# Where a planner puts 224 small modulation tiles among the weight turns of a two-block transformer kernel

## The chip, the cores and the metric

The kernel runs on one core of a Trainium2 chip. The metric is the device time of one execution in microseconds. The three runs of the kernel before took 2783.18, 2784.40 and 2785.71 us, median 2784.4 us. One profiled execution gives the trace that the text reads.

## The reference

Two transformer blocks run one after the other on 256 tokens of width 2048, all in float32. What matters here is the first block's gating and output, and the modulation vectors that both blocks need:

```python
shift, scale, gate = split(silu(c) @ w_ada + b_ada, 3)          # block 1
q, k, v, z_a, u_b, z_b, g_a, g_b = h @ w_in                      # 76 column tiles of 128
y = (sigmoid(g_a) * ((attn * silu(z_a)) @ w_pa)
     + sigmoid(g_b) * ((fourier(u_b) * silu(z_b)) @ w_pb)) @ w_out
x = rmsnorm(x + gate * y)
shift1, scale1, gate1, shift2, scale2, gate2 = split(silu(c_2) @ w_mod + b_mod, 6)   # block 2
...                                                              # block 2: projections, two kinds of attention, merge, feed-forward
```

`gate` (2048 columns) and the six vectors of block 2 are products of one vector with a 2048 x 2048 matrix each. Seven such matrices are 112 MB of weights.

## The kernel before

Activations lie feature-major in SBUF. Each weight matrix is cut into column tiles of 128, and the work is a list of **turns** (867 of them): a turn loads up to 8 weight tiles of 128 x 128 (512 KB) into one of 7 raw buffers, ScalarE (ACT) rounds them to a high part (`hi_turn`, tile `whi`, 5 buffers), VectorE (DVE) subtracts to get the low part (`lo`, tile `wlo`, 4 buffers), and TensorE (PE) multiplies both with the activations. A weight column of 16 k-tiles takes two turns; it is a **unit** with a name (`q`, `za`, `ga`, `pa`, ...). When a unit ends, ACT copies one half of its PSUM bank out (`taken`) and DVE adds the other half (`join`); only then may the unit that next uses that bank start (`claim` on PE). The banks 7 and 6 alternate from unit to unit.

The modulation matrices don't go through PE. DVE multiplies each 128 x 1024 piece by a scalar per partition and adds it into `acc` (`mod_tile`); 32 such tiles, in the order of k, make one vector, and 224 make all seven. After the last of a vector, PE sums over the partitions (`m_sum`, in the turn `plan.sums` names) and DVE folds the result into `mod`, in one burst of small instructions.

`Plan.place_mods` decides in which turn each tile lies. Every turn has a rate, the first argument of `single`; the planner adds the rates up, and each time the credit reaches one, a tile goes into that turn. After a sum it leaves a gap of three turns. The list of loads follows that order: the weights of turn t, then the tiles placed in t. Loads go out on the SP queue one by one, each into the raw buffer that the load **seven before it** used, so SP waits until DVE has finished with that one. A turn's load and a modulation tile each take one of the seven buffers.

The engines are in order. For each t the queues do this, where it touches the change:

- ACT, iteration t: `taken` of units that ended in turn t-1; then `hi_turn(t + 3)`, which waits for that load to land; then tanh and others.
- DVE, iteration t: `join` of units that ended in t-1; the fold of a vector whose sum was in t-1; `mod_tile` for the tiles placed in t+1; `lo` of turn t+2; then the gating arithmetic.
- PE, turn t: the `whi` products, small products of attention and others, the sum if there is one, the `wlo` products.

In the merge (turns 74 to 177) a loop of seven turns repeats: `ga` in two turns, `gb` in two, `pa` in two of 6 tiles each, `pb` in one of 4 tiles. The text calls them g1, g2, g3, g4, a1, a2 and b. `pa` uses the same bank as the `ga` that follows it, so g1 of the next loop can start only when `pa` has been joined, and between the end of `pa` and that start there is only turn b.

Of the kernel before, what the change touches and what calls it, by code (L numbers as in the profile page):

```python
# [147 lines left out]
class Plan:  # L148
# [18 lines left out]
    def single(self, rate, name, i, bank, rhs, weights, pieces, kt0=0, **more):  # L167
        u = Unit(name, i, bank, rhs, range(kt0, kt0 + sum(pieces)), **more)
        k = 0
        for p in pieces:  # L170
            self.turn(rate, weights[:, 128 * k:128 * (k + p)], [(u, kt0 + k + x) for x in range(p)])
            k += p
        self.finish(u)
# [18 lines left out]
    def build(self):  # L192
        src, single = self.src, self.single
        w1, w2, wp = src["w1"], src["w2"], src["w_proj"]
        two = (8, 8)
        ring = itertools.cycle((7, 6))
        bank = lambda: next(ring)
        single(0, "v", 3, bank(), "both", w1[19], two, wide=True)
        for h in range(12):
            single(.66 if h > 1 else 0.2, "q", h, bank(), "x1", w1[h], two)  # L200
            single(.66 if h > 1 else 0.2, "za", h, bank(), "x1", w1[20 + h], two)
        for g in range(4):
            single(.8, "ub", g, bank(), "x1", w1[32 + g], two)
            single(.8, "zb", g, bank(), "x1", w1[36 + g], two)

        def gates(n):
            single(.5, "ga", n, bank(), "x1", w1[40 + n], two)
            single(.5, "gb", n, bank(), "x1", w1[56 + n], two)

        gates(0)  # L210
        gates(1)
        for n in range(16):
            single(.37 if n < 15 else 0, "pa", n, bank(), "w", wp[n, :, 0:1536], (6, 6))
            single(.25 if n < 15 else 0, "pb", n, bank(), "w", wp[n, :, 1536:2048], (4,), kt0=12)
            if n + 2 < 16:
                gates(n + 2)
        for n in range(16):
# [2083 lines left out]
```

How the kernel before makes its waits and increments, by code:

```python
    def wait_ge(self, signal, value):  # L71
        return self
# [17 lines left out]
    def wait_ge(self, signal, value):  # L90
        if self.seen.get(signal, 0) < value:
            self.seen[signal] = value
            self.e.wait_ge(signal, value)
# [409 lines left out]
    def sp(e):  # L503
        e.dma_start(COLS[:, :], src["cols"]).then_inc(*lands("cols_in", "cols"))
        e.dma_start(K1[:, 0:256], src["k1"][:, 0:256]).then_inc(*lands("k1_in", "k1"))
        for i, kts in enumerate((slice(0, 2), slice(2, 6), slice(6, 10), slice(10, 14), slice(14, 16))):
            e.dma_start(XC[:, kts, :], src["xc"][:, kts, :]).then_inc(*lands(f"xc_in{i}", "xc", i))
        for r, (source, cols, shape, label) in enumerate(LOADS):
            if r >= NR:
                e.wait_ge(*on(*LOADS[r - NR][3]))
            o = raw(r)[:, 0:cols]
            if shape:
                o = o.rearrange("p (a b) -> p a b", a=shape)
            e.dma_start(o, source).then_inc(*lands(f"raw_in{r % NR}", "landed", r))
            if r == n_start - 1:
                e.dma_start(K1[:, 256:], src["k1"][:, 256:]).then_inc(*lands("k1_rest", "k1_rest"))
        for n in range(12, 16):
            e.wait_ge(*on("stored", n))
        e.wait_ge(*on("spilled"))
# [5 lines left out]
        def claim(b):  # L525
            for label in held[b]:
                e.wait_ge(*on(*label))
# [8 lines left out]
        def scale_rows(j, tiles):  # L537
# [1 line left out]
            c = 128 * GROUPS[j][1]  # L539
            if j > 1 and tiles[0] == 0:
                e.wait_ge(*on("cols_taken", j - 2 if j == 2 else j - 1))
            for i in tiles:
```

## Time and profile before

| | |
|---|---|
| median of three runs | 2784.4 us (2783.18 to 2785.71) |
| profiled execution, own time | 2783.18 us |
| its span, first to last instruction | 2781.4 us |
| around the span | 1.8 us |
| PE busy | 2757.3 us, 99% |
| DVE busy | 2049.0 us, 74% |
| ACT busy | 1458.6 us, 52% |
| granted clock of PE | 0.999 |

The span is what the trace's times are made of; a change of the span is added to the time.

### The profile page before, as it was taken

What the parts mean: (1) busy time and instruction counts of PE and PEld (TensorE: products, weight loads), DVE (VectorE), ACT (ScalarE), POOL (GpSimd) and SP (SyncE); (2) the same over time, 40 slices, a digit from 0 to 9 for tenths busy, and PEclk for the clock granted to TensorE, in tenths of its full rate; (3) what the DMA queues carried; (4) which work ended last, traced back from release to release, by engine and by line L of the source; (5) the groups of instructions that cost most, each with busy time, mean ns of one, the idle gap of its engine ahead of it and who ended that gap; (6) DMA issues with size and microseconds to landing.
All of it is one profiled execution on the core that took longest, in us unless ns stands there. A gap on an engine that the chain in (4) does not pass through costs nothing.

```text
span 2781.4 us, 42932 instructions
## 1 busy us (share of the span) xinstructions
PE 2757.3 (99%) x16354; PEld 2382.8 (86%) x16354; DVE 2049.0 (74%) x3589; ACT 1458.6 (52%) x2414; POOL 375.9 (14%) x958
## 2 busy tenths in 40 slices
PE   8999999999999999999999999999999999999999
PEld 4778888888888888888888888888888888888888
DVE  4468877878988787887878887778978555555554
ACT  3465544555566666666666444545454443444443
POOL 0014300000002424344343310000000000000000
PEclk9999999999999999999999999999999999999999
DMA  9956778888866555555555778888858555555564
GB/s 360 353 167 228 228 247 260 271 287 294 279 187 193 166 173 178 177 184 175 174 176 180 225 240 271 311 286 273 278 171 296 190 186 187 191 187 191 182 198 142
DMA packets 183582, 621.84 MB, mean 224 GB/s; under 512 B 20288, under 2 KB 28752, under 8 KB 182736
## 3 DMA queue, kind: packets, MB, share of 16 engines
q1 hardware_dynamic: 173360, 605.62, 66.1%
q10 hardware_dynamic: 10016, 13.47, 1.5%
q8 instruction: 130, 2.13, 0.3%
q14 instruction: 76, 0.62, 0.1%
HBM read 612.70 MB, written 4.21 MB: 222 GB/s over the span
## 4 chain that ended last, share of the span: by engine, by line
PE 87%; DVE 5%; ACT 3%; POOL 3%; issue 1%; DMA 1%; ACTq 0%; SPq 0%; DVEq 0%
PE ps L96 86%; POOL small L111 2%; DVE wlo L111 1%; POOL small L114 1%; PE ps L99 1%; DVE c_y L117 1%; ACT sb_l L102 1%; ACT whi L102 0%; DMA raw<-in_w_s 0%; ACT L105 0%; DMA xc<-in_xc 0%; DVE acc L117 0%; ACT sb_z L102 0%; DVE i_t L111 0%; DMA q_sw<-q_g 0%
## 5 line engine op out<-in xcount | busy, mean ns | idle before, releaser
L96 PE MATMUL ps<-act,whi 128*128 128x512 f32 (+1 forms) x6560 | 1657.4, 392 | 0.7 <-DVE act L111 0.7
L96 PEld LDWEIGHTS ps<-act,whi 128*128 128x128 f32 (+1 forms) x6560 | 1176.3, 188 | 216.2 <-issue 5.7
L111 DVE TENSOR_TENSOR wlo<-raw,whi 128x1024 fp32r<-128x1024 f32 (+3 forms) x883 | 1040.4, 1185 | 22.6 <-ACT whi L102 18.2
L102 ACT ACTIVATE whi<-raw 128x1024 fp32r<-128x1024 f32 (+3 forms) x883 | 893.9, 1027 | 194.9 <-PE ps L96 101.8
L96 PE MATMUL ps<-act,wlo 128*128 128x256 f32 (+2 forms) x6416 | 971.8, 290 | 0.0
L96 PEld LDWEIGHTS ps<-act,wlo 128*128 128x128 f32 (+1 forms) x6416 | 868.6, 190 | 55.8 <-issue 9.2
L117 DVE SCALAR_TENSOR_TENSOR acc<-raw,c_act,acc 128x1024 f32<-128x1024 f32 x210 | 268.2, 1277 | 0.0
L114 POOL TENSOR_SCALAR small<-small 128x2 f32<-128x2 f32 (+3 forms) x316 | 134.4, 425 | 937.6 <-DVE small L114 808.9
L111 POOL TENSOR_TENSOR small<-small 128x2 f32<-128x2 f32 (+1 forms) x460 | 162.7, 354 | 348.2 <-ACT u_u L102 314.0
L111 DVE TENSOR_TENSOR w_u<-w_u,ps 128x256 f32<-128x256 f32 x44 | 18.4, 420 | 95.2 <-ACT w_u L102 95.2
L117 DVE SCALAR_TENSOR_TENSOR h_res<-ps,mod,h_res 128x256 f32<-128x256 f32 x64 | 30.8, 483 | 68.3 <-PE ps L96 67.2
L111 DVE TENSOR_TENSOR w_g<-w_g,ps 128x256 f32<-128x256 f32 x44 | 18.3, 420 | 85.2 <-ACT w_g L102 85.2
L102 ACT ACTIVATE w_g<-ps 128x256 f32<-128x256 f32 x44 | 16.7, 384 | 120.7 <-PE ps L96 120.7
L102 ACT ACTIVATE w_u<-ps 128x256 f32<-128x256 f32 x44 | 16.8, 384 | 120.3 <-PE ps L96 120.3
L111 POOL TENSOR_TENSOR small<-small,small 128x4 f32<-128x4 f32 (+1 forms) x160 | 74.8, 467 | 13.1
L96 PE MATMUL ps<-m_act,whi 128*128 128x512 f32 x256 | 64.4, 393 | 1.0 <-DVE m_act L117 1.0
L96 PEld LDWEIGHTS ps<-m_act,whi 128*128 128x128 f32 x256 | 46.0, 189 | 9.6 <-DVE m_act L117 1.4
L117 DVE SCALAR_TENSOR_TENSOR d_o<-ps,mod,h_res 128x256 f32<-128x256 f32 x16 | 7.7, 483 | 58.4 <-PE ps L96 58.4
L96 PE MATMUL ps<-ff_act,whi 128*128 128x512 f32 x192 | 49.4, 392 | 0.0
L111 DVE TENSOR_TENSOR i_x<-i_x,ps 128x128 f32<-128x128 f32 x96 | 27.2, 283 | 28.0 <-PE ps L96 27.8
L117 DVE SCALAR_TENSOR_TENSOR c_y<-x_p,cols,c_y 128x256 f32<-128x256 f32 x96 | 45.8, 477 | 2.3
L102 ACT ACTIVATE x_p<-ps 128x256 f32<-128x256 f32 x48 | 18.4, 384 | 53.5 <-PE ps L96 37.9
(328 smaller groups left out, 2298.3 us busy)
## 6 DMA issues: line engine op xcount, KB each, us to landing
raw<-in_w SPq DMA_DIRECT2D x418, 512.0 KB, 4.9
raw<-in_w_mod SPq DMA_DIRECT2D x192, 512.0 KB, 4.7
raw<-in_w_gate SPq DMA_DIRECT2D x88, 512.0 KB, 4.4
raw<-in_w_up SPq DMA_DIRECT2D x88, 512.0 KB, 4.4
raw<-in_w_s SPq DMA_DIRECT2D x64, 512.0 KB, 6.6
raw<-in_w_out SPq DMA_DIRECT2D x64, 512.0 KB, 5.9
raw<-in_w_down SPq DMA_DIRECT2D x64, 448.0 KB, 4.5
raw<-in_w_ada SPq DMA_DIRECT2D x32, 512.0 KB, 5.2
```

The lines of the kernel that those rows point to most:

```text
L96: return self.e.matmul(*args, **more)
L99: return self.e.transpose(*args)
L102: return self.e.activation(*args, **more)
L111: return self.e.tensor_tensor(*args)
L114: return self.e.tensor_scalar(*args)
L117: return self.e.scalar_tensor_tensor(*args, **more)
```

## The change

The rates of the turns before the first output projection are replaced by one number, 0.58. The rates of the first ten turns and of `pa`, `pb` number 15 stay. No instruction is added or removed: 224 tiles, 7 sums and 7 folds are in both. What moves is the turn that each tile lies in, its load's place on the SP queue, and the turns of the sums.

```diff
+        early = 0.58
         for h in range(12):
-            single(.66 if h > 1 else 0.2, "q", h, bank(), "x1", w1[h], two)
-            single(.66 if h > 1 else 0.2, "za", h, bank(), "x1", w1[20 + h], two)
+            single(early if h > 1 else 0.2, "q", h, bank(), "x1", w1[h], two)
+            single(early if h > 1 else 0.2, "za", h, bank(), "x1", w1[20 + h], two)
         for g in range(4):
-            single(.8, "ub", g, bank(), "x1", w1[32 + g], two)
-            single(.8, "zb", g, bank(), "x1", w1[36 + g], two)
+            single(early, "ub", g, bank(), "x1", w1[32 + g], two)
+            single(early, "zb", g, bank(), "x1", w1[36 + g], two)
...
-            single(.5, "ga", n, bank(), "x1", w1[40 + n], two)
-            single(.5, "gb", n, bank(), "x1", w1[56 + n], two)
+            single(early, "ga", n, bank(), "x1", w1[40 + n], two)
+            single(early, "gb", n, bank(), "x1", w1[56 + n], two)
...
-            single(.37 if n < 15 else 0, "pa", n, bank(), "w", wp[n, :, 0:1536], (6, 6))
-            single(.25 if n < 15 else 0, "pb", n, bank(), "w", wp[n, :, 1536:2048], (4,), kt0=12)
+            single(early if n < 15 else 0, "pa", n, bank(), "w", wp[n, :, 0:1536], (6, 6))
+            single(early if n < 15 else 0, "pb", n, bank(), "w", wp[n, :, 1536:2048], (4,), kt0=12)
```

## Rows read from the trace of the kernel before

**Rows 1.** The page: busy time of each engine, its share of the span.

```profile
PE 2757.3 (99%) x16354; PEld 2382.8 (86%) x16354; DVE 2049.0 (74%) x3589; ACT 1458.6 (52%) x2414; POOL 375.9 (14%) x958
```

**Rows 2.** Waits of PE from 200 us on: for whom, us in total, times, longest.

```profile
PE ps L96 <- DVE i_x L111: 1.0, 2, 0.8
PE ps L96 <- DVE m_act L117: 1.0, 1, 1.0
PE ps L96 <- DVE p_m L111: 0.9, 1, 0.9
```

**Rows 3.** Chain that ended last, 430 to 700 us: start, length, what.

```profile
429.95 252.45 PE ps L96 x1456
```

**Rows 4.** Windows: attention, merge, second merge; busy per engine, clock, DMA share, GB/s.

```profile
287.10:350.86 63.76, 63.76 (x355) 53.51 (x354) 55.48 (x99) 33.22 (x60) 24.95 (x58) 1.00 0.71 229
...
554.99:672.43 117.44, 117.44 (x675) 103.13 (x673) 94.73 (x127) 60.53 (x98) 0.00 (x0) 1.00 0.87 282
...
1761.00:1961.00 200.00, 200.00 (x1159) 175.35 (x1158) 162.63 (x247) 97.41 (x157) 0.00 (x0) 1.00 0.86 287
```

**Rows 5.** Groups of DVE in the merge: busy, mean ns, idle before.

```profile
L117 DVE SCALAR_TENSOR_TENSOR acc<-raw,c_act,acc 128x1024 f32<-128x1024 f32 x40 | 51.1, 1278 | 0.0
...
L111 DVE TENSOR_TENSOR p_x<-p_x,ps 128x256 f32<-128x256 f32 x14 | 5.9, 421 | 28.5 <-ACT p_x L102 28.5
```

**Rows 6.** Timeline of one usual merge loop; its turn b starts at 592.73.

```profile
585.18 1.53 SPq L129 DMA_DIRECT2D raw<-in_w  x2
...
591.29 1.06 ACT L102 ACTIVATE whi<-raw 128x1024 fp32r<-128x1024 f32 x1 [0.93 <-DMA raw<-in_w]
...
592.73 1.09 PE L96 MATMUL ps<-act,whi 128*128 128x512 f32 x4
```

**Rows 7.** Timeline of the merge loop in which the load landed latest.

```profile
558.59 1.06 ACT L102 ACTIVATE whi<-raw 128x1024 fp32r<-128x1024 f32 x1 [1.76 <-DMA raw<-in_w]
...
559.20 1.09 PE L96 MATMUL ps<-act,whi 128*128 128x512 f32 x4
559.56 0.36 ACT L102 ACTIVATE p_x<-ps 128x256 f32<-128x256 f32 x1
...
559.96 0.42 DVE L111 TENSOR_TENSOR p_x<-p_x,ps 128x256 f32<-128x256 f32 x1 [2.16 <-ACT p_x L102]
...
560.49 0.75 PEld L96 LDWEIGHTS ps<-act,whi 128*128 128x128 f32 x4
```

**Rows 8.** Timeline of ACT: the same `whi` of g2 in five other loops.

```profile
472.38 1.06 ACT L102 ACTIVATE whi<-raw 128x1024 fp32r<-128x1024 f32 x1 [0.65 <-DMA raw<-in_w]
...
489.82 1.06 ACT L102 ACTIVATE whi<-raw 128x1024 fp32r<-128x1024 f32 x1 [1.32 <-DMA raw<-in_w]
...
506.40 1.06 ACT L102 ACTIVATE whi<-raw 128x1024 fp32r<-128x1024 f32 x1 [1.12 <-DMA raw<-in_w]
...
574.19 1.06 ACT L102 ACTIVATE whi<-raw 128x1024 fp32r<-128x1024 f32 x1 [0.61 <-DMA raw<-in_w]
...
607.55 1.06 ACT L102 ACTIVATE whi<-raw 128x1024 fp32r<-128x1024 f32 x1 [0.40 <-DMA raw<-in_w]
```

**Rows 9.** Issue to landing: merge (454:672), attention (230:345), feed-forward (2200:2600).

```profile
DMA to landing us min/median/max: 3.4/5.7/8.3
...
DMA to landing us min/median/max: 1.9/5.0/5.9
...
DMA to landing us min/median/max: 3.3/4.3/7.0
```

**Rows 10.** Timeline of DVE where the output projection waits for the last merged tile.

```profile
688.67 0.42 DVE L117 SCALAR_TENSOR_TENSOR m_act<-p_y,m_act 128x256 fp32r<-128x256 f32 x1 [0.48 <-ACT m_act L102]
```

**Rows 11.** Timeline: a sum on PE; first and last-but-next of a fold on DVE.

```profile
731.49 1.07 PE L96 MATMUL ps<-acc,k 128*32 128x256 f32 x16
...
548.00 0.18 DVE L117 SCALAR_TENSOR_TENSOR keep<-ps,cols 128x32 f32<-128x32 f32 x1
...
550.53 0.75 DVE L114 TENSOR_SCALAR acc<-raw,c_act 128x1024 f32<-128x1024 f32 x1
```

## The prediction

> **What bounds the kernel now.** I read the page first: PE is busy 99% of the span and no other engine over 74% [rows 1]. Busy is not yet bound, so the waits came next: from 200 us on PE waits 2.9 us in all, in four places [rows 2]. The chain confirms it: through the attention's end and the whole merge it is PE alone for 252 us without a break [rows 3]. So DVE work that moves from one stage to another is worth nothing in itself. Only two things can come of this change: one of those 2.9 us goes away, or a wait appears where PE has none. I therefore looked for the thinnest margin under the stages that get more tiles.
>
> **Which turns get what.** Adding the rates up by the planner's rule: between turns 10 and 50 the tiles fall from two in three turns to 0.58 per turn, 2.64 to 2.32 per head of four turns; in `ub`/`zb` from 0.8 to 0.58. There DVE has 55.5 us of work in 63.8 us [rows 4] and PE doesn't wait; less work gains nothing. In a merge loop the tiles rise from 2.99 to 7 x 0.58 = 4.06. Before, they lie in g1, g3 and a1 of every loop. After, by the same arithmetic: g1, g3, a1, b in the first two loops; g1, g3, a1, a2 in two; g1, g3, g4, a2 in three; g1, g2, g4, a2 in two; then g1, g2, g4, a2, b in one; g2, g4, a2, b in one; g2, g4, a1, b in the last three. The sums of the first three vectors move from turns 54, 119, 194 to 62, 117 (a2) and 172 (a1). The output projection keeps 12 tiles. All seven vectors are ready earlier or long before their use; later stages keep their rates, and there the pattern only shifts (sums at 339, 468, 532, 616 for 401, 487, 551, 635).
>
> **DVE in the merge.** 94.7 us in 117.4 us, seven loops: 13.5 us of 16.8 [rows 4]. One tile more holds DVE 1.2 us (1.28 long, overlapping the next by 0.08) [rows 5]: 1.07 x 1.2 = 1.3 us, 14.8 of 16.8. It fits on average. The one tight place is the join of `pa`: before it DVE is idle 28.5/14 = 2.04 us [rows 5], and the idle time starts after the join of `gb`, so only tiles in a2 and b eat into it. One of them costs nothing; both, as in two loops (before turns 147 and 154), are 2.4 us, 0.36 too many. How late may the join be? In rows 7 turn b starts at 559.20, the join ends at 560.38 and the next unit's weight load starts on time at 560.49, so about b + 1.22 is allowed (0.06 us for the semaphore). A usual join starts at b + 0.61 and ends at b + 1.03, so 0.19 is free: 0.2 us of stall in each of the two loops, **0.4 us**.
>
> **The ring of loads, the term that decides.** A tile more per loop also takes a raw buffer more. In ACT's queue the order is: `whi` of g2, which waits for its load, and only then the copy of `pa`, then DVE's join, then PE's next unit. From the start of that `whi` to the end of the join rows 7 show 558.59 to 560.38 = 1.79 us. So `whi` of g2 must start by b + 1.22 - 1.79 = **b - 0.57**. Rows 7 are at b - 0.61, with no stall and nothing left. The others, with b at 592.73 [rows 6] and a loop of about 16.78 us, by (592.73 - 559.20)/2, (17.99 for the loop with the sum, 1.07 us of PE [rows 11] and its edges): b - 1.71, - 1.05, - 1.25, - 1.76, - 1.96 [rows 8] and - 1.44 [rows 6]. ACT waits for the DMA in each: these starts are set by the landing.
>
> The load goes out when the seventh load before it is released. Before, with b, g1, its tile, a2, a1, its tile between, that is the `wlo` of g4: issue at 585.18, b' - 7.55 [rows 6]. With one tile more in the last seven it becomes the `wlo` of a1, whose release lets the next load go at 585.18 + 1.53 - 0.33 = 586.38 [rows 6]: **1.20 us later** (the loops with tiles in a1 and b or a2). Where g4 has a tile and a1 none, the seventh before is that tile, which comes between the join of `ga` and the `wlo` of a1: it ends 1.28 + 0.34 after the join starts, by the same timeline **1.53 us later** than before. In the last three loops g1 has no tile, and what stands before is 1.2 us earlier again: no loss.
>
> Taking each loop's own landing and adding this, what exceeds b - 0.57 is stall:
> first loops - 0.51, + 0.15, - 0.05: 0.06 + 0.72 + 0.52 = 1.3 us (the very first is earlier yet); the three loops of b at 575.95, 592.73, 609.51: - 0.23, + 0.09, - 0.43: 0.34 + 0.66 + 0.14, the last within the 0.2 us of DVE already counted: 1.0 us. The loop whose `pa` carries the sum gains 1.2 us of PE time and doesn't stall; but the fold (548.00 to 550.53, 2.5 us of DVE [rows 11]) now comes at the head of the next loop, in front of its `wlo`s, so the tile of g4 is released at about b + 12.2 for 10.7. The load for g2 then goes out at b' - 4.55, lands 5.8 us later, at b' + 1.3: 1.9 us of stall. Sum: **4.2 us**.
>
> I take the landing of these loads as they are, 5.4 to 6.8 us, around the merge's median of 5.7 [rows 9]. The bounds: 5.0 as in the attention [rows 9], 0.7 less, leaves the sum's loop and little else, 1.3 us; if the fuller ring makes it 0.7 longer (feed-forward, attention and merge show 4.3, 5.0, 5.7 as loads come closer [rows 9]) each of these seven loops loses 0.7 more and the very first 0.2, 9.5 us with the rest.
> The page "DMA: Bandwidth & Descriptors" of the Trainium skill, under "Anatomy of one DMA", fits a transfer as 2.0 us plus its bytes over 436 GB/s, an estimate of 3.2 us for 512 KB. The medians here are 1.1 to 2.5 us above it; by 3.2 us none of these loads would be late, and the sum would be the 0.4 us of DVE.
>
> **The seam to the output projection.** With the sum in turn 172, DVE's fold (2.5 us, and 0.5 for the shift part), a first tile (0.75) and a `wlo` stand before the join of `pa` 14: about 0.5 us late for turn 175, **+ 0.5**. The stall at 689 for the last merged tile ends with the DVE row at 688.67 [rows 10], 1.0 us [rows 2]. Of the tile in that chain the long form is replaced by the short first form (0.75 for 1.28): **- 0.55**. PE's sums cost the same wherever they are. Elsewhere I take 0, bounds - 1.9 (the waits on `i_x` and `p_m` [rows 2] gone) and + 2 (each met once more).
>
> **Sum.** 0.4 + 4.2 + 0.5 - 0.55 = + 4.6 us on a span of 2781.4, 2786.0; the execution 2783.2 + 4.6 = 2787.8. The profiled execution was 1.2 us under the median of 2784.4, so I forecast the median: 2784.4 + 4.6 = **2789.0 us**.
>
> **Rivals.**
> *Loads land in time (no stall at all).* Loads are issued as buffers come free, so a fuller ring may just spread them. For: DMA engines are busy only 0.87 in the merge [rows 4]. Against: ACT already waits for landing in each loop [rows 6 to 8]. It would be 2784.4 + 0.4 = 2784.8; it decides if the landing time of the g2 loads falls under about 5.0 us.
> *DMA becomes the bound of the merge.* Per loop 3.15 MB of weights plus 4.06 tiles of 0.524 MB = 5.27 MB in 16.78 us, 314 GB/s, for 4.71 MB, 281. The rows show 282 at share 0.87 and 287 at 0.86 [rows 4]; 282/0.87 = 324 would be the end. If it ended at 294, a loop would be 17.9 us: 13 x 1.15 = 15 us, 2799. This ends slower. Against: the same rows are no ceiling, share is not bandwidth.
> The same page, "Specifications", puts one core's limit from memory at 358 GB/s and the fabric's at 435; no row here shows a limit, and by 358 the rival fails.
> *Faster.* The gap at 689, `i_x` and `p_m` all vanish and the merge holds: 2784.4 - 2.9 = 2781.5. Nothing longer than 2.9 us is there to gain after 200 us [rows 2], and before turn 10 nothing changes. A gain over 0.2% would need a wait that the trace doesn't show.
>
> **How the numbers follow.** Landing stalls between 1.3 and 9.5 us: 0.68, and of these about 0.27 lie above + 5.6 us. No stall: 0.14. DMA-bound or stalls that build on each other, over 9.5 us: 0.14. Faster by some us: 0.04. 0.2% is 5.6 us, about what a measurement of this kernel can tell from no change. So slower 0.27 + 0.14 = 0.41 and a little for effects in later stages, 0.43; faster 0.03; same 0.54. My number sits just inside that bound, and the two outcomes are nearly even. The range reaches from the no-stall case, 2783.5, to stalls of 12 us, 2796; the likeliest case's own is 2785.7 to 2794.
>
> **What would show it.** Right: in the merge `ACT whi <- DMA` waits grow from under 1 us to 2 per loop, PE's wait on the `p_x` join appears at the start of g1, most of all in the loop after turn 117 (near 560 us), landing stays near 5.8, and the span from turn 76 to 177 grows by 4 us; attention, out1 and everything after 780 us keep their lengths. Wrong: PE's waits stay at 2.9 us (landing shorter); or PE waits at other turns, for `wlo` itself, with DVE without idle time, which would mean that the tiles' 1.3 us don't fit; or PE's `whi` products wait, a DMA-bound merge.

## The result, and the profile after

| | before | after |
|---|---|---|
| median of the comparison's runs | 2785.06 us (4 runs, 2783.18 to 2785.74) | 2801.57 us (4 runs, 2800.24 to 2803.01) |
| ratio, 95% interval | | 1.006, 1.0045 to 1.0077 |
| profiled execution, its span | 2783.18, 2781.4 us | 2796.57, 2794.7 us |

The change makes the kernel 16.5 us slower. The forecast was 2789.0 us (2783.5 to 2796): the sign was right, the size was far too small, and the time lies above the range. The profiled execution of after is 5 us faster than the median of its other runs. Their spans are 2798.4 to 2801.2 us for its 2794.7. Most show a mean granted clock of 0.997 or 0.998 where the profiled one has 0.999, but one shows 0.999 too, with a span of 2799.3 us, so the clock alone doesn't explain the distance. The last section comes back to the clock.

The busy times of after, to hold against [rows 1]. The work is the same:

```profile
PE 2759.4 (99%) x16354; PEld 2384.1 (85%) x16354; DVE 2048.6 (73%) x3589; ACT 1460.1 (52%) x2414; POOL 379.5 (14%) x958
```

PE's waits from 200 us on (for whom, us in total, times, longest), to hold against [rows 2]:

```profile
PE ps L96 <- DVE p_x L111: 5.8, 9, 1.3
PE ps L96 <- DVE i_x L111: 4.0, 4, 1.9
PE ps L96 <- ACT v_v L102: 0.7, 1, 0.7
PE ps L96 <- DVE act L111: 0.6, 1, 0.6
PE ps L96 <- DVE p_m L111: 0.5, 1, 0.5
PE ps L96 <- DVE m_act L117: 0.4, 1, 0.4
```

2.9 us have become 12.0. The wait on the join of `pa` (`p_x`) is the one that was forecast, and it is the largest. The wait on `i_x`, in the second block, was not forecast and is two thirds as large. To place them I took the start of PE's first product in some turns. Lengths of the stages in us (turn 76 to 178 is the merge; a sum on PE moved from turn 194 into the merge, 1.2 us there and 1.2 less behind it):

```
from turn    start   0     12     50    76     178   210   228    420    595
to turn      0       12    50     76    178    210   228   420    595    end
before       145.2   54.5  151.2  89.7  243.1  91.8  67.2  677.8  510.6  750.3
after        145.7   56.2  151.2  89.7  252.7  90.1  67.2  680.9  510.6  750.3
```

So the attention (12 to 50), the rest of the input projections (50 to 76) and everything behind turn 420 are unchanged to 0.1 us. The 13.3 us by which the span grew are, but for rounding, 8.4 us in the merge beside its sum, 3.1 us in turns 228 to 420, 1.7 us in turns 0 to 12, nearly all of it in turn 11, and 0.5 us ahead of turn 0, less 0.5 us behind the merge (1.7 less the sum's 1.2). Up to turn 12 the tiles lie where they lay before, so the change doesn't touch turn 11; what happened there is told in the last section.

**The merge.** Parts of the chain that ended last, after, 430 to 640 us (start, length, what), to hold against the single line of [rows 3]:

```profile
470.70 6.03 DMA raw<-in_w
476.75 1.06 ACT whi L102
478.68 17.01 PE ps L96 x96
...
522.83 6.34 DMA raw<-in_w
...
560.01 5.23 DMA raw<-in_w
...
575.81 1.21 DVE acc L117
577.03 6.54 DMA raw<-in_w
583.59 1.06 ACT whi L102
...
595.10 6.15 DMA raw<-in_w
...
612.78 6.11 DMA raw<-in_w
```

Where before had PE alone, loads of 5.2 to 6.5 us now stand in the chain. Here is one of them in the timeline of after; its turn b starts at 582.64, and the rows are the counterpart of [rows 6, 7]:

```profile
575.73 1.28 DVE L117 SCALAR_TENSOR_TENSOR acc<-raw,c_act,acc 128x1024 f32<-128x1024 f32 x1
...
577.03 0.33 SPq L129 DMA_DIRECT2D raw<-in_w  x1
...
582.64 1.09 PE L96 MATMUL ps<-act,whi 128*128 128x512 f32 x4
583.59 1.06 ACT L102 ACTIVATE whi<-raw 128x1024 fp32r<-128x1024 f32 x1 [3.32 <-DMA raw<-in_w]
584.56 0.36 ACT L102 ACTIVATE p_x<-ps 128x256 f32<-128x256 f32 x1
584.96 0.42 DVE L111 TENSOR_TENSOR p_x<-p_x,ps 128x256 f32<-128x256 f32 x1 [2.55 <-ACT p_x L102]
...
585.52 0.70 PE L96 MATMUL ps<-act,whi 128*128 128x512 f32 x2 [1.32 <-DVE p_x L111]
```

The tile of g4 holds its raw buffer until 577.01. At 577.03, b - 5.61, the load for g2 goes out. It lands 6.54 us later. ACT sits idle for 3.32 us until then, with the copy of `pa` next in its queue. `whi` starts at b + 0.95 where b - 0.57 was the latest allowed, and PE starts g1 at b + 2.88 instead of b + 1.40.

**The second block.** Around the turn with the longest new wait, ACT loads a table and computes `sb_l`; DVE waits for that, and next in DVE's queue stands the `i_x` that PE needs. First before, then after:

```profile
890.87 1.27 DVE L117 SCALAR_TENSOR_TENSOR acc<-raw,c_act,acc 128x1024 f32<-128x1024 f32 x1
...
893.24 2.00 PE L96 MATMUL ps<-act,whi 128*128 128x512 f32 x8
...
894.75 0.56 DVE L117 SCALAR_TENSOR_TENSOR sb_a<-sb_z,sb_l 128x384 f32<-128x384 f32 x1 [1.47 <-ACT sb_l L102]
...
896.03 0.49 PE L96 MATMUL ps<-i_x,l_t 128*128 128x128 f32 x2 [0.80 <-DVE i_x L111]
```

```profile
890.25 1.25 DVE L117 SCALAR_TENSOR_TENSOR acc<-raw,c_act,acc 128x1024 f32<-128x1024 f32 x1
...
904.15 2.00 PE L96 MATMUL ps<-act,whi 128*128 128x512 f32 x8
904.87 1.28 ACT L105 ACT_TABLE_LOAD   x1
906.16 0.61 ACT L102 ACTIVATE sb_l<-sb_l,k 128x384 f32<-128x384 f32 x1
906.68 1.04 ACT L102 ACTIVATE whi<-raw 128x1024 fp32r<-128x1024 f32 x1
906.81 0.56 DVE L117 SCALAR_TENSOR_TENSOR sb_a<-sb_z,sb_l 128x384 f32<-128x384 f32 x1 [2.66 <-ACT sb_l L102]
...
908.09 0.49 PE L96 MATMUL ps<-i_x,l_t 128*128 128x128 f32 x2 [1.94 <-DVE i_x L111]
```

These are turns 242 and 243. `sb_a` starts 1.51 us after PE's products in before, 2.66 us in after: the chain comes 1.15 us, about one tile, later against PE. DVE multiplies a tile one turn before the turn it lies in. In before tiles lie in turns 237 and 243, and the second starts at 890.87, in time that DVE would spend waiting for ACT (it idles 1.47 us all the same). In after the nearest lies in turn 239 and starts at 890.25, some 14 us ahead of turn 243, in front of a `wlo` and of the small steps from which ACT's inputs come; DVE is late for the chain's inputs and then idles 2.66 us while ACT works. PE's wait grows from 0.8 to 1.94 us.

### The profile page after: what moved, and what is told of

Read it like the earlier page. It is cut to its first block, busy times and chain, and to the rows that moved or that the text cites. A ratio compares the mean times of both kernels' runs of the same rounds, so it can differ in the third digit from the quotient of the medians.

```text
span 2794.7 us, 42931 instructions
## 1 busy us (share of the span) xinstructions
PE 2759.4 (99%) x16354; PEld 2384.1 (85%) x16354; DVE 2048.6 (73%) x3589; ACT 1460.1 (52%) x2414; POOL 379.5 (14%) x958
## 4 chain that ended last, share of the span: by engine, by line
PE 82%; DVE 7%; ACT 4%; POOL 3%; DMA 2%; issue 2%; ACTq 0%; SPq 0%; DVEq 0%
PE ps L96 81%; DVE wlo L111 2%; POOL small L111 2%; DMA raw<-in_w 1%; POOL small L114 1%; DVE acc L117 1%; PE ps L99 1%; ACT whi L102 1%; DVE c_y L117 1%; ACT sb_l L102 1%; DMA raw<-in_w_s 0%; ACT L105 0%; DMA xc<-in_xc 0%; ACT sb_z L102 0%; DMA q_sw<-q_g 0%
```

## The experiments

**1. ACT's order.** The copy of `pa` goes ahead of the `whi` of g2 in ACT's queue; all else as in after.

```diff
+            if after_pa(t + 2):
+                hi_turn(t + 2)          # behind the copies of turn t-1
...
-            hi_turn(t + 3)
+            if not after_pa(t + 3):
+                hi_turn(t + 3)
```

> The changed kernel, but ScalarE rounds the weights of g2 (second turn of the gate that follows pb) one iteration later, after it has copied pa out of PSUM instead of before. Loads, tiles, sums and VectorE's order stay. Theory of the ring: what stalls PE in the merge is only that the copy of pa stands behind the wait for that load, so the eleven waits of PE on the p_x join (5.6 us in the wait view, 7.1 us of length between turns 76 and 175) go but for the one at turn 175 (0.5): span 2794.7 - 6.6 = 2788. Rival, VectorE is too full in the merge: the waits stay as they are, 2794.7, since VectorE has the same work in the same order. Second rival, the merge is bound by DMA bandwidth: PE would wait for the weights themselves instead, 2794 or so.

Measured: 2794.66 us (6 runs, 2791.09 to 2796.61), ratio 1.0032 (1.0020 to 1.0044), span 2792.5. Loops 1 to 7 of the merge (loop 1 is the one whose turn b is turn 83) lose nothing any more: the join starts at b + 0.62 in each. From loop 8 on all but one lose 0.2 to 1.4 us, with DVE no longer idle before the join. Loop 11, whose turn b starts at 631.96:

```profile
633.09 1.22 DVE L111 TENSOR_TENSOR wlo<-raw,whi 128x1024 fp32r<-128x1024 f32 x1
634.22 0.41 DVE L111 TENSOR_TENSOR p_x<-p_x,ps 128x256 f32<-128x256 f32 x1
```

PE waited 3.1 us for `p_x`, against 5.8. Half of the wait sits in ACT's order, as the theory says. The rest reaches the join by another way: `wlo` waits for the late `whi` and the join waits for `wlo`. Only taking the lateness of the load away removes both. The 2788 expected was missed: in the traces the merge gets only 1.9 us shorter, 250.8 for 252.7, where the joins alone give back 3.4; 1.6 us are lost anew in turns 128 to 149, away from the joins. What PE waits for there was not followed up.

**2. An eighth raw buffer.** It is paid for with the fifth high buffer.

```diff
-NR, NH, NL = 7, 5, 4
+NR, NH, NL = 8, 4, 4
```

> The changed kernel with 8 raw buffers for 7 and, to make room, 4 buffers of high parts for 5. Theory of the ring: each load goes out one release earlier, 0.9 to 1.7 us, so the load for g2 lands at b - 1 or earlier where it landed at b - 0.3 to b + 0.9; PE's waits on the p_x join shrink from 5.6 us to under 1.5 and the merge gives back 5 to 6 us: span about 2789. Rival, DMA bandwidth: an eighth buffer doesn't help, landing gets longer by as much as issue gets earlier, 2794. Rival, VectorE too full: 2794.

Measured: 2789.85 us (10 runs, 2788.12 to 2793.88), ratio 1.0015 (1.0006 to 1.0025), span 2786.2. The merge falls from 252.7 to 245.2 us, PE waits 0.3 us for `p_x` in all, and the load for g2 goes out at b - 7.55 again. 11.7 us of the 16.5 are gone with one buffer. The theory of the ring holds. Turns 228 to 420 take 683.5 us, 2.6 more than in after; experiments 5, 9 and 10 look for the reason.

**3. The tiles of stage two put back.** In after, the tiles of the second block fall in turns 227, 233, 239, ...; before, in 225, 231, 237, ... One rate, that of `out1` number 12, brings them back.

```diff
-            single(0.5 if n < 12 else 0, "out1", ...)
+            single(0.5 if n < 12 else 0.16 if n == 12 else 0, "out1", ...)
```

> The changed kernel, with 0.16 of credit in each of the two turns of out1 number 12, so that in the second block's projections the tiles fall in the turns in which they fell before (225, 231, 237, 244 for 227, 233, 239, 246), while the merge is as in the changed kernel. Theory of the phase: the 3 us that the changed kernel lost between turns 228 and 400 come from tiles that stand in VectorE's queue just ahead of the i_x and p_m steps for which PE waits; they go, waits of PE on i_x fall from 4.0 to about 1 us, span 2794.7 - 3 = 2791.7. Rival, those 3 us are from the sum and fold at turn 339 or from the run: 2794.7, with the waits on i_x still 4.

Measured: 2797.46 us (5 runs, 2796.67 to 2798.29), ratio 1.0041 (1.0027 to 1.0055), span 2796.5: 4.1 us less than after. Turns 228 to 420 take 678.9 us. The stage does what was expected, the time less well. The merge took 257.7 us in this execution, with the same order of work as in after's 252.7: its loads happened to land later, up to 7.1 us, and behind a wait of 2.7 us the clock fell (0.72 in the window 567 to 573 us), 1.7 us of the 5.

**4. The merge's rates alone.** The attention and `ub`, `zb` get their old rates, 0.66 and 0.8; the merge keeps 0.58.

> Only the merge part of the change: gates, pa and pb at 0.58, attention at 0.66 and ub/zb at 0.8 as before. Theory of the ring: what was changed ahead of the merge is worth nothing, and the merge loses as in the changed kernel or somewhat more, since more loops have a tile in g4 or in both a2 and b: merge + 6 to 10 us, span 2791 to 2798 with the phase of stage two as it falls. Rival, the thinner attention is what costs or gains: then the time goes back to the 2785 of before or well over 2800.

Measured: 2803.71 us (4 runs, 2800.04 to 2805.8), ratio 1.0062 (1.0047 to 1.0077), span 2803.9. As slow as after, and above the 2791 to 2798 expected of the span: the clock fell four times in it, and its merge took 256.3 us. Turns 12 to 76 take the same 240.9 us in before, after and here. Taking tiles out of the first stages has no part in the loss.

**5. Ring and place together.** Edits 2 and 3.

> The changed kernel with both suspected causes taken away: an eighth raw buffer (and four high buffers instead of five), and the tiles of stage two back in the turns in which the kernel before has them. If the ring of loads and the position of stage two's tiles are the whole loss, the stages from turn 76 to 178 take 243 to 246 us, those from 228 to 420 678 to 681 us, and the time is 2786 us (2784 to 2788). If the fuller VectorE or the second sum in the merge costs by itself, it stays at 2789 us or above.

Measured: 2788.23 us (11 runs, 2786.57 to 2790.66), ratio 1.0012 (1.0004 to 1.0021), span 2785.7; merge 245.1, turns 228 to 420 681.6 us. Just above the range expected of the first theory, 2784 to 2788: something was left, in the second block.

**6 and 7. Where the tiles of a loop lie.** The same four tiles in each merge loop as in after, once all in the gate turns (6), once three in a1, a2 and b and one in g4 (7).

```diff
-            single(early, "ga", n, ...)                    # gb alike
+            single(1, "ga", n, ...)                        # in 6
+            single(0.25, "ga", n, ...)                     # in 7
...
-            single(early if n < 15 else 0, "pa", n, ...)   # pb alike
+            single(0 if n < 15 else 0, "pa", n, ...)       # in 6
+            single(1 if n < 15 else 0, "pa", n, ...)       # in 7
```

> The changed kernel with the same four tiles in each merge loop, but all in the four gate turns (rate 1 there, 0 in the turns of p_a and p_b). If it is the position in the ring of the tile ahead of the load for the loop's second gate turn that costs, this load is issued as in the kernel before, p_x is waited for by less than 2 us in all, the merge (turns 76 to 178) takes 244 to 247 us and the time is 2788 us (2785 to 2791). If it is the number of tiles (VectorE's work, the DMA queues' bytes), the merge stays at 251 us or above and the time at 2794 us or above.

> The changed kernel with the same four tiles in each merge loop, but three of them in the turns of p_a and p_b and one in the last gate turn. If the position in the ring costs, the load for the loop's second gate turn is late in all fourteen loops, p_x is waited for by 1 to 2 us in nearly each, the merge takes 258 us or more and the time is 2806 us (2800 to 2815). If it is the number of tiles, the merge takes 250 to 254 us as in the changed kernel and the time is 2796 to 2802 us.

Measured: 2796.15 us (4 runs, 2792.95 to 2797.76), ratio 1.0040 (1.0026 to 1.0054), for the sixth, and 2795.78 us (4 runs, 2794.63 to 2799.49), ratio 1.0042 (1.0029 to 1.0056), for the seventh. The merge takes 247.5 and 247.7 us. The first half of the theory held: the number of tiles isn't the cost, since the same four per loop cost 5 us less when they lie elsewhere. The time fell by as much, 5.4 and 5.8 us, but not to the 2788 expected of the sixth: both lost more in turns 228 to 420 (683.9 and 685.0 us). The second half, a seventh run at 2806 us, was wrong, and usefully so. In the seventh the load for g2 isn't the latest of all, it goes out at b - 6.66 in 12 of 13 loops, and b - 6.66 leaves 6.09 us until b - 0.57. Those loads landed in 5.32 to 6.23 us; in 11 of those 12 loops PE lost 0.05 us at most, in the one at 6.23 it lost 0.12. In the sixth it goes out at b - 6.35 to b - 6.06 in nine loops, room for 5.5 to 5.8 us; these loads took 5.12 to 6.05 us, and PE lost nothing in five of the loops and 0.10 to 0.55 us in four. In all of them the loss is what the landing exceeds b - 0.57 by, to 0.1 us; what I had wrong was the time of issue.

The one large stall of the seventh is of another kind. Behind the sum of turn 122 its fold and three tiles meet before one join, and DVE works through them (the chain, 560.13 to 564.05):

```profile
561.15 1.28 DVE acc L117
562.43 1.14 DVE wlo L111
563.57 0.34 DVE p_x L111
```

It costs 2.7 us and is what a stall by the fuller VectorE would look like: no DMA in this part of the chain.

**8. The place alone.** The kernel before, with the tiles of stage two two turns later.

```diff
-            single(0.5 if n < 12 else 0, "out1", ...)
+            single(0.5 if n < 11 else 0.34 if n == 11 else 0, "out1", ...)
```

> The kernel before with one edit: the tiles of stage two fall two turns later (227, 233, 239 instead of 225, 231, 237), where they fall in the changed kernel. If that position is what stage two lost, turns 228 to 420 take 680 to 681 us instead of 677.8, everything else stays, and the time is 2787.5 us (2786.5 to 2788.5). If stage two's loss in the changed kernel came from something else, the time is 2785 us (2784.3 to 2785.8).

Measured: 2790.69 us (11 runs, 2787.47 to 2792.45), ratio 1.0021 (1.0012 to 1.0030), span 2786.6. PE's waits from 200 us on:

```profile
PE ps L96 <- DVE i_x L111: 3.5, 4, 2.0
PE ps L96 <- DVE m_act L117: 1.0, 1, 1.0
```

The merge is unchanged (243.1 us), turns 228 to 420 take 683.5 us. The place of these tiles alone costs 5.8 us, where I had expected 2.7 from after's stage. In this trace the stage lost 5.7 us, and 1.7 of them are the clock: the window 896 to 902 us, behind the wait of 1.95 us (columns: length, busy us of PE, PEld, DVE, ACT, POOL, granted clock, DMA share, GB/s):

```profile
896.00:902.00 6.00, 4.54 (x18) 4.02 (x19) 5.75 (x12) 3.67 (x6) 0.00 (x0) 0.72 0.37 126
```

**9 and 10. Buffers.** Eight raw, five high and three low buffers with the tiles of stage two put back (9), and the kernel before with eight, four, four (10).

> As the run with eight raw buffers and the tiles of stage two put back, but with five high and three low buffers instead of four and four, in the same memory. That run was 3.4 us above the kernel before, with turns 228 to 420 at 681.6 us. If the missing fifth high buffer costs there, this one shows 678 to 679 us for these turns and 2785 to 2786.5 us of time. If something else of the change is left, it stays at 2788 us; if the fourth low buffer matters more, it is above that.

> The kernel before with eight raw and four high buffers instead of seven and five, nothing else. Control for the ring runs: if the fourth high buffer costs by itself, turns 228 to 420 take 680 to 682 us instead of 677.8 and the time is 2787 to 2789 us. If eight raw buffers are simply better, the merge stays at 243.1 us, nothing is lost later, and the time is 2784 to 2785 us. PE doesn't wait in this kernel's merge, so no gain of over 1 us is there to be had.

Measured: 2784.99 us (11 runs, 2783.44 to 2788.06), ratio 0.9998 (0.9989 to 1.0007), for the ninth, and 2786.22 us (11 runs, 2784.97 to 2788.46), ratio 1.0005 (0.9996 to 1.0014), for the tenth. The ninth has the change's rates in full and the time of the kernel before. Its turns 228 to 420 take 678.8 us, those of the tenth 680.1: the missing high buffer was what was left in the fifth run, there 2.8 us. The tenth shows this in its stage (2.3 us in a trace that was its slowest execution) and not in its median, which I had expected at 2787 to 2789. The kernel before was not run with eight, five and three; its merge has no wait of PE to gain from it, but that nothing else would is not shown. The chain of the ninth through the merge, to hold against [rows 3], and its waits:

```profile
429.89 245.21 PE ps L96 x1421
```

```profile
PE ps L96 <- DVE i_x L111: 1.9, 3, 0.9
PE ps L96 <- DVE p_m L111: 1.3, 2, 0.9
PE ps L96 <- DVE m_act L117: 0.4, 1, 0.4
PE ps L96 <- DVE p_x L111: 0.3, 1, 0.3
```

It also settles the rival of the DMA engines. Here are the windows 441 to 694 us of after and 441 to 684 us of the ninth (the last three columns are the granted clock, the DMA share and GB/s):

```profile
441.00:694.00 253.00, 247.07 (x1419) 214.07 (x1418) 215.49 (x347) 123.80 (x204) 0.00 (x0) 1.00 0.87 301
```

```profile
441.00:684.00 243.00, 242.67 (x1406) 211.42 (x1406) 213.63 (x345) 122.68 (x202) 0.00 (x0) 1.00 0.90 308
```

With one buffer more the same loads move at 308 GB/s and PE doesn't wait; 301 GB/s with waits was no limit.

**11. The ring alone.** After with eight, five, three, the tiles of stage two as the change puts them.

> The changed kernel with eight raw, five high and three low buffers, and nothing else: the one edit that takes the landing waits of the merge away. If the loss is the ring of loads plus the place of stage two's tiles, and the two add up, the merge (turns 76 to 178) takes 245 us, turns 228 to 420 take 681 us as in the changed kernel, with PE's wait of 1.9 to 2.0 us at turn 252, and the time is 2790.5 us (2788.5 to 2792), since the place alone cost the kernel before 5.8 us. If the place costs only the 3.1 us by which the profile's stage grew, it is 2788 us. If the waits of stage two came from the merge's lateness, they are gone and the time is 2785 us.

Measured: 2789.20 us (11 runs, 2787.82 to 2791.62), ratio 1.0013 (1.0003 to 1.0022), span 2786.0. The merge takes 245.2 us, PE waits 1.95 us at turn 243 (the expectation has its number wrong), and turns 228 to 420 take 683.8 us, with the clock at 0.72 behind that wait as in the eighth run. So the loss closes: 2801.6 us of after, less 12.4 with the ring, less 4.2 more with the place, is 2785.0, the time before. Measured each against the runs of the kernel before beside them, the three are at + 16.5, + 3.9 and - 1.2 us, which gives 12.6 for the ring and 5.1 for the place. No version was faster than the kernel before; the 2.9 us of its waits leave little to win.

## Why the prediction failed, by its steps

In short: the wait and its path were forecast rightly, the term of the ring was too small (4.2 us; 7.1 in the trace, and 12.4 in the medians of after and experiment 11), and "Elsewhere I take 0" was wrong (3.1 us in the trace, 5.8 us in the median of experiment 8).

**Which turns get what, and the mechanism: right.** The wait appears at the start of g1, on the join, behind a `whi` that waits for a load that is issued late. Experiments 1, 2 and 11 show each link. The loop named as the worst, the one behind turn 117, lost 1.23 us and was second, behind the next one with 1.49.

**The bound b - 0.57: right**, to 0.1 us in every loop of after and of experiments 6 and 7 in which the load is what is late.

**"Taking each loop's own landing and adding this": the step that failed.** It gave 4.2 us; the stalls of loops 1 to 11 are 7.1, and each costs 0.07 us more in the turn behind it. The table has PE's stall in us in fourteen loops (loop 1 has its turn b at turn 83), with the landing time of the load two turns behind b, that for g2, in both traces. Loop 14 is the seam, where that load isn't late. The forecast row is without the 0.2 us of DVE in each of loops 10 and 11:

```
loop               1     2     3     4     5     6     7     8     9     10    11    12    13    14
forecast           0     0.06  0.72  0.52  0     0     1.9   0.34  0.66  0.14  0     0     0     0.5
after              0.44  0.38  0.25  0.62  1.05  0     1.23  1.49  0.83  0.79  0.04  0     0     0.48
landing before     5.55  5.81  6.48  6.28  4.87  5.43  6.13  5.60  6.09  5.57  5.78  6.77  5.71  3.36
landing after      6.23  6.03  5.90  6.27  6.34  5.97  5.23  6.54  6.15  6.11  5.51  4.96  5.03  3.98
issue after, b -   6.35  6.20  6.20  6.20  5.85  7.07  4.55  5.60  5.87  5.87  6.10  6.23  6.68  8.42
```

Two things are in it. A load's landing time isn't its own: loop 5 had 4.87 us before and was counted as safe, and took 6.34 after. The mean over loops 1 to 13 is 5.85 and 5.87, so the landing did stay as it was, as a mean; but a stall is what exceeds a bound, and when the bound on the landing (5.0 to 5.8 us in ten of the thirteen loops) goes through the middle of the scatter, the loops below it give nothing back. Experiment 3, with the same order, had a mean of 6.35 us and a merge 5 us longer still. Second, the time of issue in loops 5 and 8 to 10 was b - 5.6 to b - 5.9, 1.7 to 1.8 us later than before, where I took 1.20 or 1.53, and in loops 11 to 13, where I took "no loss", it was 0.9 to 1.5 us later. These last cost next to nothing only by luck: loop 12's load landed in 4.96 us, and with the 6.77 us of before it would have cost 1.1. The second thing weighs more. The landings of before with the times of issue of after give 6.8 us of stall, an estimate from the two rows of the table and b - 0.57; the exchange of the landings adds the last 0.3. I had allowed up to 9.5 us for the merge by longer landings. The 8.4 measured in the trace lie within that, and 2784.4 + 8.4 = 2792.8 us would have been inside the range. The medians say more: experiment 3, with the ring's loss and without that of the second block, took 2797.46 us, so the ring, with what the clock adds, takes the time past 2796 without the second block.

The rule that I set beside it, the page "DMA: Bandwidth & Descriptors" of the Trainium skill under "Anatomy of one DMA", gives an estimate of 3.2 us for these loads. By it no load would be late. The page states its fit per DMA and for DMAs issued by GpSimd, and these are issued by SP, which the prediction didn't say. After's loads for g2 took 4.96 to 6.54 us in loops 1 to 13 and nine of them were late, so the fit doesn't hold for the loads of this merge.

**DVE's two full loops, + 0.4: too high.** With the join at b + 0.88, 0.04 to 0.05 us were lost in such a loop and 0.07 in the turn behind it (experiments 5, 7 and 9), 0.24 us for two.

**The seam + 0.5 and the last merged tile - 0.55: right**, 0.48 and - 0.53 us.

**"Elsewhere I take 0": wrong.** "Later stages keep their rates, and there the pattern only shifts" was read as harmless. The shift by two turns costs 3.1 us of PE's waits in the trace and, by experiment 8, 5.8 us in the median. My bound there, + 2, was made from waits that existed. It left out that a tile which moves to another side of a chain through ACT and DVE can make a wait of 1.94 us where there was one of 0.80, and new ones where there was none.

**The clock: not thought of.** It accounts for the 1.7 us in turn 11, and probably for a part of the distance from the profile's + 13.3 us to the median's + 16.5.

**The rivals.** Loads in time: refuted by PE's waits. DMA-bound: refuted by experiment 9, which moves 308 GB/s where the rival had the end at 294; it is a coincidence that its 2799 lay nearest to the result. Faster: no.

What stays open is how the 12.4 us that the ring costs in the medians divide: 7.5 us are the merge's 252.7 less 245.2 in the profiled executions, and the rest probably lies in executions whose loads land later and whose clock falls more often. That isn't shown: one execution of each kernel was traced.

## What to carry to other kernels

A planner that spreads work evenly over one engine's time spreads something else unevenly: here each tile also takes a slot in a ring of loads, and the slot decides when a load seven places later goes out. Before moving such work, write down for each load the time from its issue to its latest harmless landing, and compare that with the whole scatter of landing times, not with each load's own time in one trace. And when a shift reaches stages that "keep their rates", go through the tightest chain of each of them turn by turn; a pattern that only shifts can still lose.

## What the runs showed of the hardware

PE's granted clock can fall to half, from 2.4 to 1.2 GHz, behind a wait of PE of some 2 us, and does so in some executions and not in others of the same work. Behind the wait for `prob_t` near 197 us, which every version has (1.95 to 2.46 us), the same eight products took 1.97 us in before and 3.41 us in after:

```profile
196.89 1.97 PE L96 MATMUL ps<-prob_t,v_tok 128*128 128x256 f32 x8 [2.46 <-ACT prob_t L102]
```

```profile
197.53 3.41 PE L96 MATMUL ps<-prob_t,v_tok 128*128 128x256 f32 x8 [2.44 <-ACT prob_t L102]
```

The window 196 to 202 us has a granted clock of 1.00 in before and of 0.72 in after:

```profile
196.00:202.00 6.00, 5.11 (x26) 4.36 (x27) 5.99 (x8) 3.72 (x7) 0.00 (x0) 1.00 0.46 152
```

```profile
196.00:202.00 6.00, 4.47 (x17) 3.85 (x18) 4.86 (x7) 2.32 (x4) 0.00 (x0) 0.72 0.41 137
```

0.28 of 6 us is 1.7 us lost. In the thirteen traces of this study, between 50 and 2770 us, PE was idle for 1.8 us or longer 25 times (1.81 to 2.71 us); behind 13 of these waits, and nowhere else, the clock fell. So a wait of about 2 us that a change adds has a second price of 1.7 us, paid about every other time. This fits the eighth run, where the place of stage two's tiles costs more than its waits: its eleven executions show a mean clock of 0.997 or 0.998, those of the kernel before beside them 0.998 or 0.999.
